# Six 64-row expert tiles in the first layer, experts sorted by load on the chip, and another order of the steps between the layers

## The reference, cut to what matters

```python
for l in range(DEPTH):                       # DEPTH = 2
    mod = silu_c @ ada_w[l] + ada_b[l]       # shifts, scales and gates, also for the context
    o_lat, o_ctx = even_mixer(...) if l == 0 else odd_mixer(...)
    x = x + g1 * o_lat                       # ctx likewise in layer 0
    # layer 0: 512 tokens, layer 1: the 256 latent tokens alone
    x = x + g2 * hier_moe(modulate(x, sh2, sc2), ...)

def hier_moe(x, ...):
    # top-1 of 4 groups, then the top-2 of its 4 experts, with weights that sum to the group's probability
    y = jnp.zeros_like(x)
    for e in range(16):
        hdn = jax.nn.silu(x @ w_gate[e]) * (x @ w_up[e])      # 1024 -> 512
        y = y + combine[:, e:e + 1] * (hdn @ w_down[e])       # 512 -> 1024
    return y
```

## Time and profile before

| what | value |
|---|---|
| three runs, median (lowest to highest) | 986.64 us (981.43 to 987.10) |
| profiled execution: span, its only time | 988.0 us |
| TensorE busy | 943.3 us, 95% |
| VectorE / ScalarE / GpSimd busy | 618.0 / 182.4 / 114.0 us |
| moved by DMA | 312.01 MB |
| expert phase of layer 0, from the first gate product | about 333 to 598 us |
| between the layers, to the first query product | about 598 to 641 us |
| expert phase of layer 1 | about 770 to 978 us |

### The profile page before, as it was taken

How to read it: one execution, slowest core, us unless ns; L and a number is a source line. 1 busy time by engine, 2 the same in 40 slices (tenths; PEclk the granted TensorE clock), 3 DMA queues, 4 the chain that set the end, 5 groups by cost and what they waited for, 6 DMA issues and landing times.

```text
span 988.0 us, 19912 instructions
## 1 busy us (share of the span) xinstructions
PE 943.3 (95%) x8018; PEld 566.7 (57%) x8018; DVE 618.0 (63%) x1502; ACT 182.4 (18%) x343; POOL 114.0 (12%) x172
## 2 busy tenths in 40 slices
PE   4999999999998999999999998999998999999996
PEld 2443433457445788989888874445645545554442
DVE  2100699869545697776767645648514887777763
ACT  3010022155014110000000003316603100000001
POOL 7010100100500100000000214100010110000000
PEclk9999999999999799999999999999999999999999
DMA  9999957356655999999999957945225999999993
GB/s 314 372 414 414 396 208 303 108 217 261 192 182 181 346 359 358 421 427 428 428 426 428 421 180 274 372 144 199 89 89 185 365 427 424 423 412 427 423 430 161
DMA packets 58781, 312.01 MB, mean 316 GB/s; under 512 B 9725, under 2 KB 19709, under 8 KB 41440
## 3 DMA queue, kind: packets, MB, share of 16 engines
q1 hardware_dynamic: 43632, 277.88, 70.3%
q0 software_dynamic: 9920, 21.20, 6.8%
q10 hardware_dynamic: 5168, 12.06, 3.3%
HBM read 302.76 MB, written 17.25 MB: 324 GB/s over the span
## 4 chain that ended last, share of the span: by engine, by line
PE 79%; DVE 8%; DMA 5%; another core or an unknown queue 2%; issue 2%; ACT 2%; SPq 1%; ACTq 0%; DVEq 0%; POOLq 0%
PE ps L667 51%; PE ps L1123 11%; PE ps L682 3%; PE ps L1011 3%; PE ps L1169 3%; PE ps L1263 2%; DMA ring<-in_moe_w_gate 2%; DMA ring<-in_ada_w 2%; DVE ar L2331 1%; PE ps L1514 1%; DMA ar<-h_rows,sm 1%; DVE ar L2302 1%; SPq L549 1%; PE ps L947 1%
## 5 line engine op out<-in xcount | busy, mean ns | idle before, releaser
L667 PE MATMUL ps<-ring,ar 128*32 128x384 f32 (+6 forms) x3852 | 473.6, 464 | 4.4 <-issue 2.3
L667 PEld LDWEIGHTS ps<-ring,ar 128*32 128x32 f32 (+2 forms) x3852 | 188.0, 120 | 128.5 <-issue 75.7
L1123 PE MATMUL ps<-ring,ar 128*32 128x128 f32 x1488 | 166.5, 274 | 0.0
L1123 PEld LDWEIGHTS ps<-ring,ar 128*32 128x32 f32 x1488 | 163.5, 111 | 3.1
L2302 DVE STREAM_TRANSPOSE ar<-ar 32x256 f32<-32x256 f32 x304 | 132.2, 435 | 6.4 <-DMA ar<-h_rows,sm 2.1
L667 PE MATMUL ps<-xh,ring 128*128 128x512 f32 x256 | 114.0, 597 | 1.4 <-ACT xh L1563 1.4
L667 PE MATMUL ps<-ring,xh 128*128 128x512 f32 x192 | 84.6, 595 | 1.0 <-ACT xh L1574 0.9
L667 PEld LDWEIGHTS ps<-xh,ring 128*128 128x128 f32 x256 | 47.4, 190 | 62.6 <-issue 60.4
L2344 DVE TENSOR_TENSOR ar<-ar,ps 128x384 f32<-128x384 f32 (+2 forms) x33 | 15.9, 482 | 106.8 <-PE ps L1123 63.2
L2480 DVE SCALAR_TENSOR_TENSOR ar<-ar,cpar 128x512 f32<-128x512 f32 x120 | 79.6, 743 | 0.0
L2331 DVE STREAM_TRANSPOSE ar<-ar 32x64 f32<-32x64 f32 x256 | 60.4, 236 | 4.5
(11 more groups left out here) (392 smaller groups left out, 915.9 us busy)
## 6 DMA issues: line engine op xcount, KB each, us to landing
ring<-in_moe_w_gate SPq DMA_DIRECT2D x30, 2048.0 KB, 14.8
ring<-in_moe_w_up SPq DMA_DIRECT2D x30, 2048.0 KB, 12.6
ring<-in_moe_w_down SPq DMA_DIRECT2D x30, 2048.0 KB, 15.9
ring<-in_ada_w SPq DMA_DIRECT2D x24, 2048.0 KB, 14.3
ring<-in_even_w_in SPq DMA_DIRECT2D x4, 2048.0 KB
y_rows<-ar POOLq DMA_DIRECT2D x17, 384.0 KB, 10.6
ring<-in_odd_w_in SPq DMA_DIRECT2D x3, 2048.0 KB, 24.7
y_rows<-ar ACTq DMA_DIRECT2D x16, 288.0 KB, 8.8
```

Source lines behind the costliest of these rows:

```text
L667: return nc.tensor.matmul(o, l, r, start=start, stop=stop)
L1123: m = nc.tensor.matmul(ps[96:128, bank, g * P:(g + 1) * P], xgT[:, p, c, 32 * g:32 * g + 32], w[:, c, 3 * P:HID], start=c == 0 and g == 0, ...
```

## The change

`FIXED = 4` places stay as they are. The other 12 experts are now sorted by their number of rows, ascending: places 4 to 9 (`SMALL`) get tiles of 64 rows in layer 1's form, places 10 to 15 get tiles of 96 rows. A small tile with more than 64 rows would overflow. `MAXOV` goes from 15 to 16, and six more transfers clear the unused 32 rows of each small place in `y_rows`.

- `router(0)`: the old search for an overflowing expert goes; new is a sort by pairwise comparison (`key_e`, `fewer`, `place_e`), before the first row lists.
- `overflow_counts(0)` is longer and is moved behind `hidden_t` of expert 0; `weights(0)` is moved ahead of the wait for the row lists.
- TensorE makes the row lists (`rows_numbered(0)`) between gate 0 and up 0 instead of ahead of gate 0.
- The loops over expert places of layer 0 become straight code on all engines, since tiles now differ in shape.
- Between the layers: `mix_rows(2)` takes the place of one of the three `keep_clock` matmuls, `mix_rows(3)` comes after the key-value product of tile 0, the next tile's rows are turned ahead of the last two of the eight chunks of a key-value product, and VectorE and ScalarE follow that order.

The core of the diff:

```diff
+FIXED = 4
+SMALL = range(FIXED, 10)
+SMALL_CAP = 64
+LESS = CAP[0] - SMALL_CAP
...
+        def small_place(l, e):
+            return l == 0 and e in SMALL
+
+        def hid_width(l, e):
+            return P if narrow(l, e) else HID // 2 if l or small_place(l, e) else 3 * P
...
         def store_y(tile, p, done):
             to = y_rows.rearrange("(t s) n -> t s n", s=CAP[0])[tile, :, :]
+            if small_place(0, tile):
+                for h in range(2):
+                    nc.scalar.dma_start(to[0:SMALL_CAP, 512 * h:512 * h + 512], yb[64 * h:64 * h + 64, p, 0:512]).then_inc(done, 16)
+                return
...
+            def small_down(p, w):
+                for c in range(HC):
+                    for h in range(2):
+                        for k in range(2):
+                            o = 512 * h + 256 * k
+                            m = mm(ps[64 * h:64 * h + 64, 5 + k, 0:256], hidT[:, p, c % 2, 64 * (c // 2):64 * (c // 2) + 64],
+                                   w[c // 2][:, c % 2, o:o + 256], c == 0, c == HC - 1)
+                return m
...
-                    do_product(l, p, up, blk(i)).then_inc(sem("block_used"), 1)
+                    do_product(1 if small_place(l, e) else l, p, up, blk(i)).then_inc(sem("block_used"), 1)
...
             def experts(l):
                 pe.wait_ge(sem("h2_act"), NT + NLAT if l else NT)
                 gate_up(l, 0, 0, at["g", l, 0], 0, False)
+                if l == 0:
+                    rows_numbered(0)
                 gate_up(l, 0, 0, at["u", l, 0], 0, True)
...
             def odd_mixer():
                 near_and_last()
-                keep_clock(0, (512, 512, 512))
+                mix_rows(2)
+                keep_clock(0, (512, 512))
...
                     for c in range(KC):
+                        if kind == "kv" and j + 1 < NT and c == 6:
+                            odd_rows_turned(j + 1)
...
-                    if kind == "kv" and j + 1 < NT:
-                        odd_rows_turned(j + 1)
-                    if kind == "kv" and j + 2 < NT:
-                        mix_rows(j + 2)
+                    if (kind, j) == ("kv", 0):
+                        mix_rows(3)
...
                 for j in range(NT):
                     gated(j)
-                    if j == 0:
-                        weighted(1)
+                    if j + 1 < NT:
+                        weighted(j + 1)
                     row_norm(2, j)
-                    if j == 0:
-                        last_added(1)
+                    if j + 1 < NT:
+                        last_added(j + 1)
                     modulated(1, 0, j, 3)
-                    if 0 < j < NT - 1:
-                        weighted(j + 1)
-                        last_added(j + 1)
...
+                held = ps[:, 1, 256 + 16 * n:272 + 16 * n]
+                if l == 0:
+                    far = NEXP - FIXED
+                    link(V.scalar_tensor_tensor(key_e[:, 0:far], held[:, 0:far], float(NEXP), cst[:, C_E:C_E + far], ALU.mult, ALU.add))
+                    fewer = cmp_c[:, 0:far * NEXP].rearrange("p (e k) -> p e k", e=far)
+                    link(V.tensor_tensor(fewer, key_e.unsqueeze(1).to_broadcast([P, far, NEXP]),
+                                         key_e[:, 0:far].unsqueeze(2).to_broadcast([P, far, NEXP]), ALU.is_lt))
+                    V.tensor_reduce(ov_most, held[:, 0:far], AX_X, ALU.max)
+                    link(V.tensor_reduce(place_e[:, 0:far], fewer, AX_X, ALU.add))
+                    V.tensor_scalar(ov_from, ov_most, float(CAP[0]), float(NEXP - 1), ALU.is_le, ALU.add)
+                    link(V.tensor_scalar(less_e[:, 0:far], place_e[:, 0:far], float(SMALL.stop), float(LESS), ALU.is_lt, ALU.mult))
+                    link(V.tensor_tensor(held_e, less_e, held, ALU.add))
+                    held = held_e
...
             def overflow_counts(l):
...
+                if l == 0:
+                    by, count, ids = place_e[0:1, :], nov[0:1, :], cst[0:1, C_E:C_E + NEXP]
+                    a, b = a[0:1, :], b[0:1, :]
+                    begun = tile_hot[0:1, 0:16 * MAXOV].rearrange("p (i k) -> p i k", k=16)
+
+                    def each(row):
+                        return row.unsqueeze(1).to_broadcast([1, 16, 16])
+                    link(V.tensor_tensor(tv, each(by), by.unsqueeze(2).to_broadcast([1, 16, 16]), ALU.is_ge))
+                    V.tensor_tensor(begun, each(by), ids.unsqueeze(2).to_broadcast([1, 16, 16]), ALU.is_equal)
+                    link(V.tensor_scalar(ov_none, ov_most, float(CAP[0]), None, ALU.is_le))
+                    link(V.tensor_tensor(tv, tv, each(count), ALU.mult))
+                    link(V.tensor_reduce(a, tv, AX_X, ALU.add))
+                    link(V.tensor_scalar(a, a, ov_none[0:1, :], None, ALU.add))
+                    V.tensor_tensor(begun, begun, each(ids), ALU.mult)
+                    link(V.tensor_reduce(te[:, 0:1], a, AX_X, ALU.max))
+                    V.tensor_copy(ov_n, te[:, 0:1])
+                    link(V.tensor_tensor(b, a, count, ALU.subtract))
+                    link(V.tensor_reduce(key_e[0:1, :], begun, AX_X, ALU.add))
+                    link(V.tensor_copy(order, key_e[0:1, :]))
+                    V.tensor_tensor(tv, each(a), steps, ALU.is_gt)
+                    link(V.tensor_tensor(begun, each(b), steps, ALU.is_gt))
+                    link(V.tensor_tensor(tv, tv, begun, ALU.subtract))
+                    link(V.tensor_tensor(tv, tv, each(ids), ALU.mult))
+                    link(V.tensor_reduce(te, tv, AX_X, ALU.add))
+                    V.tensor_copy(ov_e, te).then_inc(sem("routed"), 1)
+                    return
...
             def experts(l):
-                if l == 0:
-                    overflow_counts(0)
-                    weights(0)
-                else:
+                if l == 1:
                     weights(1)
...
                 hidden_t(l, 0, 0)
                 if l == 0:
+                    overflow_counts(0)
                     weights_scaled(0)
                     rows_placed()
...
+                for t in SMALL:
+                    pool.dma_start(y_rows[t * CAP[0] + SMALL_CAP:(t + 1) * CAP[0], :], zeros[0:LESS, :]).then_inc(sem("y_zero"), 16)
```

More of the change, by code:

```diff
@@ L1 @@
 from contextlib import ExitStack
+from functools import lru_cache
 import numpy as np
@@ L32, with overflow_tiles, most_overflow_tiles @@
 NARROW = 32
-FULL = 2 * NT * P // (CAP[0] + NARROW + 1)
-MAXOV = 2 * FULL + (2 * NT * P - FULL * (CAP[0] + NARROW + 1) > CAP[0])
+FIXED = 4
+SMALL = range(FIXED, 10)
+SMALL_CAP = 64
+LESS = CAP[0] - SMALL_CAP
+def overflow_tiles(place, count):
+    count += LESS if place in SMALL else 0
+    return 0 if count <= CAP[0] else 1 + -(-max(0, count - CAP[0] - NARROW) // CAP[0])
+@lru_cache(None)
+def most_overflow_tiles(place, rows, least):
+    if place == NEXP:
+        return 0
+    if place == FIXED:
+        least = 0
+    best = 0
+    for count in [least] + [c for k in range(11) for c in (65 + 96 * k, 97 + 96 * k, 33 + 96 * k) if c > least]:
+        rest = NEXP - place if place >= FIXED else 1
+        if count * rest <= rows:
+            best = max(best, overflow_tiles(place, count) + most_overflow_tiles(place + 1, rows - count, count if place >= FIXED else 0))
+    return best
+MAXOV = 16
+assert MAXOV >= most_overflow_tiles(0, 2 * NT * P, 0)
 assert MAXOV >= (2 * NLAT * P - 2) // CAP[1]
@@ L279, in hybrid_dit @@
             gm=1, ge=4, gx=4, gs=1, pg=1, ohg=4, rank=20, m12=2, dd=1, ex=1, dn=1, rd=1, M12=32, MM=20, t12=32, lower=32,
-            ek=2, e0=2, dk=2, q=2, r12=2, kk=2, ke=2, sl=2, ne=2, xk=2, tile=2, py=2, pb=2).items()}
+            ek=2, less=2, none=2, r12=2, kk=2, ke=2, sl=2, ne=2, xk=2, tile=2, py=2, pb=2).items()}
+        place_e, key_e, less_e, held_e = (small(NEXP) for _ in range(4))
         nov, inc, inc2 = (small(NEXP) for _ in range(3))
@@ L310, in hybrid_dit @@
         order = small(NEXP)[0:1, :].bitcast(I32)
-        first_ov, place_hit, place_first = small(NEXP), small(NEXP)[0:1, :], small(NEXP)[0:1, :]
-        ov_place, ov_none, ov_from, ov_expert, ov_minus = (small(1) for _ in range(5))
+        ov_most, ov_none, ov_from = (small(1) for _ in range(3))
         assert 27 + NTL <= 60 and MAXOV <= NEXP
@@ L1664, in experts @@
                 step(1, 1)
-                with act.Fori(0, NEXP // 2 - 2) as t:
-                    step(2 * t + 2, 0)
-                    step(2 * t + 3, 1)
+                if l == 0:
+                    for e in range(2, NEXP - 2):
+                        step(e, e % 2)
+                else:
+                    with act.Fori(0, NEXP // 2 - 2) as t:
+                        step(2 * t + 2, 0)
+                        step(2 * t + 3, 1)
                 step(NEXP - 2, 0)
@@ L1817, in odd_mixer @@
                 row_root(2, 1)
-                y_scaled(3)
                 for u, (kind, j) in enumerate(OUNITS[:-1]):
+                    if kind == "kv" and j + 1 < NT:
```

(26 more changed lines are left out.)

118 lines of the change are left out of this document (61 added, 57 removed).

## The result

**Of 20 runs each, the changed kernel has a median of 988.60 us (985.16 to 991.61) and the kernel before 985.28 us (980.44 to 989.93); the three runs that the forecast stood on had 986.64 us.** The ratio is 1.0033, 95% interval [1.0017, 1.0048]: 3.3 us slower, no change by the bound of 1%. The profiled execution took 991.56 us with a span of 989.6 us. Three of the 105 runs of the kernel before that stand beside the experiments took 1239 to 1647 us at a mean clock of 0.56 to 0.75, and are left out of every comparison.

A forecast was written before the change was run, and what follows sets the result against it. TensorE was busy 95% but living on a lead, with DMA transfers the next bound 4 us away in layer 0. +2.7 us in the expert phase and -2.4 between the layers gave +0.3, so 987 us, range 978 to 995.

The forecast's parts named there:

- The transfers bind: Layer 0's expert phase: DMA delivers a block in 5.58 us, so 31.3 us less TensorE time is worth only what transfers allow.
- The wait that the change adds: `overflow_counts(0)` ahead of `rows_placed`: 6.3 us of VectorE work, `mix_src` at 363.5 us, TensorE standing still 5.9 us.
- The start: Ahead of the expert phase: first row lists 1.7 us later, gate 0 near 332.6 us, gate 1 about 1.6 us later.
- The clock after the wait: TensorE after standing still for `mix_src`: a fall of its clock costs 1.7 us, bounds 0 and 3.3.
- The end of the phase: Layer 0's last expert blocks: down 14 lands near 581.0 us and ends at 586.7, 2.7 us later than before.
- It keeps its distance: Behind down 14: narrow tile, down 15, stores and gathers follow at the same distance as before.
- Loops made straight: Layer 0's expert loops as straight code: worth nothing, since looped and straight steps both take 15.66 us.
- Between the layers: From first key-value product to first query product, 28.3 us before: 2.4 us less, bounds 0 and -4.
- Counts hidden: Rival: VectorE's idle time hides the counts, so no 5.9 us wait or clock loss; -7.3 us, 979 us; chance 0.15.
- Transfers don't bind: Rival: DMA can go faster when asked, so TensorE's 31.3 us come through; 962 us; chance 0.07.
- Paced stretch loses its clock: Rival: waiting for DMA in places 7 to 9, TensorE drops to 1.2 GHz; 994 us; chance 0.10.
- Small tiles don't fit: Rival: a small place has over 64 rows, adding an overflow step of about 32 us; 1019 us; chance 0.01.

The follow-up runs named there:

- large form: Changed kernel with the six small places computed and stored in the large form (31.3 us more for TensorE): 990.93 us, ratio 1.0060 to the kernel before.
- half gates: Changed kernel with the gate weights of places 4 to 9 loaded by half, 6.3 MB less moved: 978.18 us, ratio 0.9938 to the kernel before.
- dense waits: The gap and turn kernel with a dummy matmul ahead of each block of places 6 to 9: 982.96 us, against 981.89.
- gap and turn: The counts in gap kernel with `rows_turned` of expert 1 also ahead of VectorE's wait for the row lists: 981.89 us, ratio 0.9985 to the kernel before.
- order alone: Kernel before with only the new order of the steps between the layers: 982.60 us, ratio 0.9970 to the kernel before.
- tiles alone: Changed kernel with the old order between the layers, so sort, small tiles and straight loops alone: 990.09 us, ratio 1.0046 to the kernel before.
- gap, large: The counts in gap kernel with the six small places computed and stored in the large form: 984.62 us, ratio 1.0017 to the kernel before.
- counts in gap: Changed kernel with `overflow_counts(0)` right behind `weights(0)`, where VectorE stood idle: 981.79 us, ratio 0.9974 to the kernel before.

## Why the prediction was right, point by point

The forecast was no change at 987 us; the time is 988.6, and the sum of +0.3 us measured +3.3 [1.7, 4.7]. The mechanism held and several sizes were off. That 987 lies so near 988.6 is in part luck: it stood on a median of three runs that was 1.4 us above that of 20, so the sum missed by 3.0 us and the time by 1.6.

- **The transfers bind.** Right: 426 GB/s before and after, the waits for DMA from about 440 us on, and three experiments (large form, half gates, dense waits). Gate 15 was used from 568.3 us before, as I had it, but that is one step and 1.84 us behind 550.81, not two steps less a block.
- **The wait that the change adds.** Right in place and time: `mix_src` at 363.6 us for 363.5. TensorE stood 4.7 us for 5.9, because it got there 1.4 us later than I had it.
- **The start.** The first lists came at 325.22 us, 1.45 later for 1.7. Gate 1 began at 348.35 us, 2.9 later for 1.6, and my reason for it was mostly wrong. VectorE's turning held it by about 0.5 us at most: gap and turn took that away and won nothing. Gate 0 began 0.9 us earlier but took 8.2 us for 6.8, since more of it ran at half clock: the mean over 330 to 345 us is 0.77 both before and after, but before the 3.5 us of numbering stood in the slow part. The numbering behind it took another 1.9 us.
- **The clock after the wait.** 1.7 us taken, 2.4 in `weights_turned`, within the bounds. The Trainium skill, "TensorE: Matmul & The Clock Gate", section "HAM oscillation", has waits for data bring a cold restart each time, in a kernel whose waits are long. The 4.7 us wait agrees. The waits in the paced stretch here are shorter, 1.6 to 2.8 us, and do so only in part: the second profile of the changed kernel waited 13.4 of 40 us from 440 us on with a granted clock of 1.00, the first 10.5 us with 0.91.
- **The end of the phase.** The mis-sized term: down 14 was to land at 581.0 us and end at 586.7; it landed at 584.3 and ended at 589.4, +5.4 us for +2.7. Gate 4 was issued 10.15 us later for 9.2, and the 2.2 us of y don't show against the kernel before (209.2 us from gate 4 to the landing of down 14, 209.3 after). They show only against the large form in the new code (210.9 and 211.6). That form moves as much y as the old code, which has 209.2 (and 207.9 in order alone), so the new code costs the transfers some 2 us elsewhere. Part of it is in the trace. From 10 to 20 us behind the issue of gate 4, ahead of the full stretch, DMA was 84% full before (81% in order alone), and 69 to 72% in the kernels with the new code, large form or small (half gates aside). The rows are of the kernel before and of the changed one:

```profile
374.80:384.80 10.00, 10.00 (x166) 7.82 (x159) 8.99 (x22) 0.60 (x1) 0.18 (x1) 1.00 0.84 311
384.95:394.95 10.00, 10.00 (x166) 7.83 (x159) 9.15 (x22) 0.60 (x1) 0.06 (x1) 1.00 0.71 252
```

That is 1.3 us of DMA time. Over the 209 us behind gate 4's issue the queue of instructions moved 0.34 MB for 0.20 (0.44 in the large form), by estimate 0.3 to 0.6 us at 426 GB/s. Why DMA is less full there, and whether the straight loops are why more instructions are moved, no run tests. By times, tiles alone is +4.5 us.
- **It keeps its distance.** Wrong for the profile that I summed against. Behind down 14 that execution has gaps that end on nothing visible:

```profile
584.88 0.41 PE L667 MATMUL ps<-ring,ar 128*32 128x128 f32 x4 [0.33 <-issue]
585.61 0.27 PE L667 MATMUL ps<-ring,ar 128*32 128x128 f32 x1 [0.32 <-issue]
586.32 3.70 PE L667 MATMUL ps<-ring,ar 128*32 128x128 f32 x113 [0.43 <-issue]
...
598.30 0.62 PE L667 MATMUL ps<-ring,ar 128*32 128x256 f32 x3 [0.82 <-issue]
```

From the last load to near it takes 46.3 us there, and 41.5 to 41.7 in every one of the other 13 profiles, among them order alone, which has the same code up to there. So 4.8 us of that profile belong to one execution. That is why the changed kernel's profile is only 1.0 us behind at near, when the phase itself lost 5.4. That execution was also slower than it was taken for: the 988.0 us are a span, and in the changed kernel the span of 989.6 us belongs to a time of 991.56, so its time was by estimate about 990 us, where the slowest of its 20 runs lies.
- **Loops made straight.** Worth nothing, as taken: from wt to near 238.3 us with the loop (order alone) and 238.3 without (gap, large). The Trainium skill, "Runtime: NRT & Kernel Launch", section "Instruction fetch mechanics", has a taken branch force a fetch stall when its target has not been fetched; no run here shows one in these loops.
- **Between the layers.** -2.4 us, bounds 0 and -4. By times -3.0 us (order alone, interval 0.5 to 5.4), in the profiles without a fall of the clock there -0.8 to -2.7, depending on how late VectorE is for tile 1. The bound had named tiles 2 and 3.
- **The rivals.** Counts hidden: did not happen, but counts in gap shows that it could have. It needed another place in VectorE's order, and gave 5.6 to 6.8 us by medians (4.6 to 5.8 by ratios) for the 7.6 worked out. Transfers don't bind: refuted. Paced stretch loses its clock: the clock fell to 0.91, not under 0.8, and dense waits shows no cost of it. Small tiles don't fit: no such step in the trace.

## What to carry to other kernels

Where landing times grow while DMA is full, cheaper multiplying mostly lengthens the queue: 31.3 us of it were worth 2 to 4 us, and 6.3 MB less moved were worth 8 to 10. When work goes into an engine's fixed order, list every waiter behind it, not the first: put by one place further back it kept half of its price, put into that engine's own idle gap it cost nothing that shows. And before a sum is made against one profile, compare it with a second one of the same code, since 4.8 us of the profile used here were that execution's own.

## What the runs showed of the hardware

- The mean granted clock of a run goes with its time, in the same kernel: 33 runs of the kernel before reach from 0.985 (988.5 to 989 us) to 0.996 (980.7 us), with exceptions (991.0 us at 0.987). That spread is over twice the 3 us between the two kernels.
- Dense dummy matmuls in waits hold the clock at 1.00 where it was 0.89, while DMA beside them stays at 426 GB/s. TensorE's work did not slow the transfers there.
- With half blocks among the loads the queues were equally full from 400 to 440 us (1.00) but moved 398 GB/s for 420. The loss lies ahead of 413 us; from 413 to 433 us, with half blocks still coming, it is 424 GB/s, so that their size is the cause isn't shown.
- In one execution of the changed kernel the clock was 0.50 from 604.8 to 615 us with TensorE busy for 10.1 of the 10.2 us. In another of the same program it was 1.00 from 598 to 616 us.
